# Prompt attention's exponentials over up to 1024 columns instead of 512

## The chip, the cores and the metric

One core of a Trainium2 chip runs the whole program. The metric is its device time in microseconds (us), from the profiler's and the runtime's clocks. Engines are named as in the profile: PE is TensorE (matmuls and transposes; PEld its weight loads), ACT is ScalarE, DVE is VectorE, POOL is GpSimd, SP is SyncE, which issues DMAs.

## What is computed

One layer of a streaming encoder, over 2048 prompt tokens and, separately, 64 sample tokens with a cache of 4096. Two groups of 8 heads look at the same tokens. The first is stick-breaking attention (a sigmoid of the scores and a running product instead of a softmax), the second is latent attention with a plain softmax over a mask in chunks of 64. The part that the change touches is the softmax of the prompt:

```python
s = (jnp.einsum('bqhn,bkhn->bhqk', q_nope, k_nope)
     + jnp.einsum('bqhr,bkr->bhqk', q_rope, k_rope)).astype(jnp.float32)
s = s * ((MLA_NOPE_DIM + MLA_ROPE_DIM) ** -0.5)
visible = (k_pos[None, :] // CHUNK) <= (q_pos[:, None] // CHUNK)
s = jnp.where(visible, s, jnp.finfo(jnp.float32).min)
p = jax.nn.softmax(s, axis=-1)
return jnp.einsum('bhqk,bkhv->bqhv', p.astype(v.dtype), v)
```

## The kernel before

The program is a row of phases: set-up, input projection, queries, keys, prompt attention (`prompt_attention_phase`, L1124), and a tail with the sample's attention and the output projection. A barrier of all engines closes each phase.

Prompt attention loops over 8 heads, and in each over two jobs: job 0 is stick-breaking, job 1 latent attention. The 2048 queries are 16 tiles of 128, in 4 groups (`g`, 4 tiles `i` each). A query tile's scores are computed against the keys that it may see, in chunks of 512 keys, so that group g has g+1 chunks per tile. This gives 4 x (1+2+3+4) = 40 chunks per job (`JOB`), 80 slots per head (`HEAD`), counted by `m`. Slots 0 to 39 are job 0, 40 to 79 job 1.

A second work runs 20 slots (`LEAD`) behind the scores: at slot `t` the finished weights of one block of 128 keys, for the 4 query tiles of a group, are transposed on TensorE (L1666), copied to a high part by ScalarE (`whi`, L1431), the remainder made a low part by VectorE (L1473), or by GpSimd (L1592) from a whole copy that ScalarE makes for it (L1436), and multiplied with the values 4 slots later (L1623). GpSimd has the low part where `on_pool(t)` holds: t of 60 to 79 and 0 to 19, but not where t % 4 is 3.

In each slot every engine runs its own fixed program, and semaphores join them. TensorE: the 4 transposes of t, the value matmuls of t - 4, then the scores of m = t + 20 (L1649 to L1655) into one of 2 banks, for which the scan or the maximum of m - 2 must be done. ScalarE: the copies of t, at the end of a group `finish` (L1424), then `chunk(h, m)`: in job 0 the sigmoid of chunk m (L1389), in job 1 the exponentials that `exps_at(m)` lists (L1396). VectorE: the low part of t - 1, then for m the scan (L1496, job 0) or the copy out of the bank with a running maximum (L1506, job 1), and after a tile's last chunk `negtop` (L1511).

An exponential needs the maximum of its whole row, so it runs in place on the tile `probs[g][i]` in SBUF after the tile's last chunk: piece c, of 512 columns, at one slot after the last chunk plus c. Slots at or over 80 fall into the next head: there the distance from 80 is halved, so that the four pieces of the last tile come as two at 80 and two at 81. At these, m is 0 and 1 of the next head, and ScalarE's `chunk` puts them ahead of that head's first sigmoids, both of which it runs at m = 1:

```python
if m < 2 and not (isinstance(h, int) and h == 0):
    for g, i, c in exps_at(HEAD + m):
        exp(h - 1, g, i, c)
    if m == 0:
        return
    sigmoid(h, 0)
```

Each piece gives its sum to its own column of `sums` (zeroed once at the start), which VectorE adds up over all 4 columns (L1518). A tile's last piece raises `exp_done`; TensorE waits for the 4 tiles of a group before that group's first transpose (L1663).

Of the kernel before, what the change touches and what calls it, by code (L numbers as in the profile page):

```python
# [11 lines left out]
P = 128  # L12
# [1111 lines left out]
def prompt_attention_phase(nc, outer, d, s, ps):  # L1124
# [4 lines left out]
    G = 4  # L1129
    GROUPS = 2 * G  # L1130
    CH = 512
    JOB = 40
    HEAD = 2 * JOB
# [4 lines left out]
    ADD = 4  # L1138
    PARTS = 4
    EVEN = 113  # L1140
    with ExitStack() as ctx:
        sb = lambda name, shape, dt=F32: ctx.enter_context(nc.sbuf_tensor(name, shape, dt))
        sm = Sems(nc, ctx, "pa")
# [45 lines left out]
        def upto(n):  # L1189

            g = n % G
            return JOB * (n // G) + 2 * (g + 1) * (g + 2)
# [5 lines left out]
        def chunk_of(m):  # L1198
            n, r = group_of(m)
            return n, *divmod(r, n % G + 1)  # L1200

        def keys_of(n, i, c):

            g = n % G
            kc = c if n >= G else g - c
            return kc * CH, (4 * g + i + 1) * P - kc * CH if kc == g else CH

        def first_query(t):
            n, i = group_of(t)
            return max(0, i - 4 * (n % G)) * P  # L1210

        def on_pool(t):

            return (t + LEAD) % HEAD < JOB and t % 4 != 3
# [3 lines left out]
        def low_of(h, t):  # L1218

            pool = on_pool(t)  # L1220
            per = POOLS if pool else HEAD - POOLS
            return (pool_lo if pool else dve_lo), per * (h + 1) + sum(on_pool(x) == pool for x in range(t + 1))
# [6 lines left out]
        def ends_at(t):  # L1229

            t = (t - LAG) % HEAD
            return next((n for n in range(GROUPS) if upto(n) % HEAD == t), None)

        def past(h, n):
            return h - 1 if n == GROUPS - 1 else h

        def is_none(h):
            return isinstance(h, int) and h < 0
# [13 lines left out]
        def chunk_at(h, t, last):  # L1252

            if t + LEAD < HEAD:
                return h, t + LEAD
            return (None, 0) if last else (h + 1, t + LEAD - HEAD)
# [13 lines left out]
        with nc.Block() as block:  # L1270

            @block.sync
            def _(sp):
# [31 lines left out]
                def load_v(h, job):  # L1305
# [9 lines left out]
                    if job == 0:  # L1315

                        sp.dma_start(step_v[:, 1:], v[P - 1:T - 1].rearrange("(j p) c -> p j c", p=P)).then_inc(v_loaded, 16)
                        sp.dma_start(step_v[1:EVEN, 0], v[0:EVEN - 1]).then_inc(v_loaded, 16)
                        sp.dma_start(step_v[EVEN:P, 0], v[EVEN - 1:P - 1]).then_inc(v_loaded, 16)

# [59 lines left out]
            @block.scalar  # L1380
            def _(act):
                act.sem_inc(taken, 2)
                act.sem_inc(whole_done, POOLS)
                def sigmoid(h, m):
                    n, i, c = chunk_of(m)
                    _, width = keys_of(n, i, c)
                    act.wait_ge(scores, HEAD * h + m + 1)
                    bank = ps[:, m % NS, 0:width]
                    act.activation(bank, bank, ACT.Sigmoid, scale=-SB_SCALE).then_inc(sig_done, 1)  # L1389

                def exp(h, g, i, c):
                    at = 4 * g + i
                    if c == 0:
                        act.wait_ge(negtop_done, 16 * h + at + 1)
                    keys = slice(c * CH, min((at + 1) * P, (c + 1) * CH))
                    x = act.activation(probs[g][i][:, keys], probs[g][i][:, keys], ACT.Exp, scale=MLA_SCALE,  # L1396
                                       bias=negtop[:, at:at + 1], accum_out=sums[:, at, c:c + 1])
                    if c == g:
                        x.then_inc(exp_done, 1)

                def exps_at(m):

                    due = [(m_last + 1 + c, g, i, c) for g in range(G) for i in range(4)
                           for m_last in (upto(G + g) - (3 - i) * (g + 1) - 1,) for c in range(g + 1)]
                    return [(g, i, c) for when, g, i, c in due if (when if when < HEAD else HEAD + (when - HEAD) // 2) == m]

                def chunk(h, m):
                    if h is None:
# [7 lines that stand above are left out]
                    if m < JOB:  # L1416
                        sigmoid(h, m)
                    for g, i, c in exps_at(m):
                        exp(h, g, i, c)

                def finish(h, n):
                    act.wait_ge(mixed, NW + HEAD * h + upto(n))
                    act.wait_ge(stored[n % 2], 16 * (G * h + n // 2))
                    act.activation(out[:, n % 2, :], ps[:, 6 + n % 2, :], ACT.Copy).then_inc(taken, 1)  # L1424

                def step(h, t, last):
                    q0 = first_query(t)
                    act.wait_ge(turned, HEAD * (h + 1) + t + 1)
                    act.wait_ge(mixed, HEAD * h + t + 1)
                    bank = ps[:, NS + t % NTB, q0:]  # L1430
                    act.activation(whi[:, t % NW, q0:], bank, ACT.Copy).then_inc(hi_done, 1)  # L1431
                    if on_pool(t):
                        before = (h, t - 4) if t >= 4 else (h - 1, HEAD + t - 4)
                        if on_pool(before[1]):
                            act.wait_ge(*low_of(*before))
                        act.activation(whole[:, t % 4, q0:], bank, ACT.Copy).then_inc(whole_done, 1)  # L1436
                    n = ends_at(t)
                    if n is not None and not is_none(past(h, n)):
                        finish(past(h, n), n)
                    if last and t + LEAD in (HEAD, HEAD + 1):  # L1440
                        for g, i, c in exps_at(t + LEAD):
                            exp(h, g, i, c)
                    chunk(*chunk_at(h, t, last))

                for m in range(LEAD):
                    chunk(0, m)
                act.wait_ge(own_loaded, 16)
                act.wait_ge(hide_made, 2)
                act.activation(own_tile[:], probs[3][2][:, 0:CH], ACT.Copy)
                act.activation(hide[:], probs[3][2][:, CH:CH + P + CHUNK], ACT.Copy).then_inc(const_done, 1)  # L1450
                steps_in_turn(act, step)
                finish(HEADS - 1, GROUPS - 1)
# [1029 lines left out]
```

## Time and profile before

| | us |
|---|---|
| median of 3 runs | 2436.88 (2432.28 to 2438.32) |
| the profiled execution | 2436.27 |
| its span, first to last instruction | 2434.2 |
| busy: TensorE, VectorE, ScalarE, GpSimd | 2196.4, 1344.1, 1323.2, 895.9 |
| prompt attention | from about 1016 to 2029 |

The span is what lies between the program's first and last instruction; the run's time has 2.07 us more around it. A row of a time line gives an instruction's start, its length, and in brackets how long its engine had been idle before it and what ended that. Rows of ScalarE overlap: one instruction ends after the next has begun, so what an instruction occupies is read from start to start. An exponential with a sum is two instructions, ACTIVATE and ACTIVATION_READ_ACCUMULATOR.

### The profile page before, as it was taken

Reading aid. Unit: us, or ns where it says so; the run is one execution under the profiler, and the core shown is the slowest. Engines: PE = TensorE matmul, PEld = TensorE weight load, DVE = VectorE, ACT = ScalarE, POOL = GpSimd, SP = SyncE. Lnnn points to the kernel's source line nnn. Section 1 sums busy time; section 2 is a strip of 40 time slices with the busy share of each in tenths; the row PEclk is TensorE's granted clock in tenths of the full one; section 3 lists DMA queues with packets and bytes.
Section 4 is the critical chain, followed back from the end, with each engine's and each line's share of the span. In section 5 each row is a group of like instructions: output and inputs, shape, how many; then the busy total and the mean of one; then the engine's idle time right before and its main releaser. Section 6 shows DMA issues by size and latency. Waiting matters only on the chain. (4 is left out here: it accounts for less than half of the span.)

```text
span 2434.2 us, 39766 instructions
## 1 busy us (share of the span) xinstructions
PE 2196.4 (90%) x12100; PEld 1837.8 (75%) x12100; DVE 1344.1 (55%) x2780; ACT 1323.2 (54%) x2872; POOL 895.9 (37%) x922
## 2 busy tenths in 40 slices
PE   6999997999988899789999999999999993999998
PEld 1888886999988577567777777777777782887876
DVE  3232322200138333387878787878787873667783
ACT  2232322211123333278888888888888884467553
POOL 0000000000000000265848484848484825656673
PEclk9999999999989999889999999999999996999999
DMA  7433342322347799943333323333323224676772
GB/s 274 136 98 99 96 123 72 126 72 93 115 155 198 247 320 312 259 90 83 78 84 69 87 67 87 70 87 71 86 70 89 47 64 123 189 227 185 218 211 87
DMA packets 296944, 320.16 MB, mean 132 GB/s; under 512 B 88641, under 2 KB 221788, under 8 KB 291826
## 3 DMA queue, kind: packets, MB, share of 16 engines
q1 hardware_dynamic: 292002, 302.00, 44.2%
q10 hardware_dynamic: 2880, 9.05, 1.0%
q0 software_dynamic: 1904, 7.41, 0.8%
q8 instruction: 51, 0.84, 0.1%
q14 instruction: 107, 0.88, 0.1%
HBM read 199.09 MB, written 110.90 MB: 127 GB/s over the span
## 5 line engine op out<-in xcount | busy, mean ns | idle before, releaser
L1431 ACT ACTIVATE pa_whi<-banks 128x512 fp32r<-128x512 f32 (+3 forms) x640 | 345.3, 540 | 99.1 <-PE banks L1666 80.3
L1666 PE MATMUL banks<-ident,pa_p 128*128 128x128 f32 x2176 | 356.4, 280 | 2.2 <-ACT pa_p L1396 2.2
L1649 PE MATMUL banks<-pa_khi,pa_qst 128*128 128x512 f32 (+3 forms) x640 | 261.0, 408 | 84.4 <-DVE pa_p L1496 76.5
L1592 POOL TENSOR_TENSOR pa_wlo<-pa_whole,pa_whi 128x512 fp32r<-128x512 f32 (+2 forms) x240 | 277.7, 1171 | 137.9 <-ACT pa_whole L1436 137.5
L1666 PEld LDWEIGHTS banks<-ident,pa_p 128*128 128x128 f32 x2176 | 269.2, 144 | 61.7 <-issue 5.2
L1623 PE MATMUL banks<-pa_whi,pa_vst 128*128 128x512 f32 (+3 forms) x640 | 286.3, 447 | 4.2 <-POOL pa_wlo L1592 3.0
L1496 DVE TENSOR_TENSOR_SCAN pa_p<-banks,pa_p,pa_zero 128x512 f32<-128x512 f32 x192 | 246.3, 1283 | 72.3 <-ACT banks L1389 65.7
L1473 DVE TENSOR_TENSOR pa_wlo<-banks,pa_whi 128x512 fp32r<-128x512 f32 (+3 forms) x400 | 234.8, 587 | 30.7 <-ACT pa_whi L1431 30.7
L1649 PEld LDWEIGHTS banks<-pa_khi,pa_qst 128*128 128x128 f32 x640 | 125.7, 196 | 159.1 <-DVE pa_p L1496 136.8
L1650 PE MATMUL banks<-pa_klo,pa_qst 128*128 128x512 f32 (+3 forms) x640 | 243.3, 380 | 0.0
L699 POOL DMA_DIRECT2D gate_ada<-in_ada_w_dram x2 | 1.8, 884 | 642.8 <-DVE qu_wlo L755 642.8
L1623 PE MATMUL banks<-pa_wlo,pa_vst 128*128 128x512 f32 (+3 forms) x640 | 237.9, 372 | 0.0
L1396 ACT ACTIVATE pa_p<-pa_p,pa_negtop 128x512 f32<-128x512 f32 (+2 forms) x320 | 208.8, 654 | 4.9 <-DVE pa_negtop L1511 4.3
L1389 ACT ACTIVATE banks<-banks 128x512 f32<-128x512 f32 (+3 forms) x320 | 172.0, 540 | 66.9 <-PE banks L1650 61.4
L653 PE MATMUL banks<-co_hhi,co_whi 128*128 128x352 f32 x576 | 188.1, 327 | 18.0 <-DVE co_h L620 9.8
L481 PE MATMUL banks<-nat_whi,pr_hhi 128*128 128x512 f32 (+5 forms) x544 | 196.1, 360 | 6.8 <-DVE pr_hlo L425 6.8
L481 PE MATMUL banks<-nat_wlo,pr_hhi 128*128 128x512 f32 (+5 forms) x544 | 195.3, 359 | 0.0
L481 PE MATMUL banks<-nat_whi,pr_hlo 128*128 128x512 f32 (+5 forms) x544 | 195.1, 359 | 0.0
L653 PE MATMUL banks<-co_hhi,co_wlo 128*128 128x352 f32 x576 | 186.0, 323 | 0.0
L1506 DVE TENSOR_SCALAR_CACHE_REDUCE pa_p<-banks,pa_top 128x512 f32<-128x512 f32 (+2 forms) x192 | 124.5, 648 | 30.4 <-PE banks L1652 17.9
L1650 PEld LDWEIGHTS banks<-pa_klo,pa_qst 128*128 128x128 f32 x640 | 127.2, 199 | 13.8
L1436 ACT ACTIVATE pa_whole<-banks 128x512 f32<-128x512 f32 (+2 forms) x240 | 136.6, 569 | 1.5 <-POOL pa_wlo L1592 1.5
(260 smaller groups left out, 5171.6 us busy)
## 6 DMA issues: line engine op xcount, KB each, us to landing
scratch_sb_kT<-ke_kT SPq DMA_DIRECT2D x12, 1024.0 KB, 8.9
scratch_mla_kT<-ke_nT SPq DMA_DIRECT2D x12, 1024.0 KB, 5.2
scratch_mla_v<-ke_v SPq DMA_DIRECT2D x12, 1024.0 KB, 5.4
scratch_gatesT<-co_gates SPq DMA_DIRECT2D x12, 704.0 KB, 11.3
ada<-in_ada_w_dram SPq DMA_DIRECT2D x4, 2048.0 KB, 11.9
pr_x<-in_x_prompt_dram SPq DMA_DIRECT2D x16, 512.0 KB, 18.1
scratch_hT<-pr_hT SPq DMA_DIRECT2D x16, 512.0 KB, 5.1
ke_k<-in_cache_sb_k_dram SPq DMA_DIRECT2D x8, 1024.0 KB, 7.7
```

The source lines that it names most:

```text
L481: mm = pe.matmul(ps[0:rows, 2 + g, 0:n], h[:, b, c, 0:rows], s[w][:, c, c0:c0 + n], start=(c == 0 and k == 0), stop=(c == DC - 1 and k == 2))
L653: mm = pe.matmul(ps[:, ct % RING, 0:N], w[:, c, ct * P:(ct + 1) * P], h[:, c, :], start=(c == 0 and k == 0), stop=(c == DC - 1 and k == 2))
L1389: act.activation(bank, bank, ACT.Sigmoid, scale=-SB_SCALE).then_inc(sig_done, 1)
L1396: x = act.activation(probs[g][i][:, keys], probs[g][i][:, keys], ACT.Exp, scale=MLA_SCALE, bias=negtop[:, at:at + 1], accum_out=sums[:, at ...
L1431: act.activation(whi[:, t % NW, q0:], bank, ACT.Copy).then_inc(hi_done, 1)
L1473: dve.tensor_tensor(wlo[:, t % NW, q0:], ps[:, NS + t % NTB, q0:], raw(whi[:, t % NW, q0:]), ALU.subtract).then_inc(dve_lo, 1)
L1496: dve.tensor_tensor_scan(tile[:, first_key:first_key + width][:, ::-1], scored[:, ::-1], given, start, ALU.mult, ALU.max).then_inc(scan_do ...
L1592: pool.tensor_tensor(wlo[:, t % NW, q0:], whole[:, t % 4, q0:], raw(whi[:, t % NW, q0:]), ALU.subtract).then_inc(pool_lo, 1)
L1623: mm = pe.matmul(ps[:, 6 + n % 2, q0:], vst[job][:, j, :], w[:, t % NW, q0:], start=(job == 1 and j == 0 and k == 0), stop=(j == 4 * g + 3 ...
L1649: pe.matmul(bank, qst[job][:, q], khi[job][:, keys], start=True, stop=False)
L1650: mm = pe.matmul(bank, qst[job][:, q], klo[job][:, keys], start=False, stop=(job == 0))
L1666: y = pe.transpose(ps[:, NS + t % NTB, x * P:(x + 1) * P], probs[g][x][:, i * P:(i + 1) * P], s["ident"][:])
```

## The change

A piece of an exponential covers up to 1024 columns (`WIDE`) instead of 512. A tile of group 0 and 1 then has one piece, a tile of group 2 and 3 two. Piece c still comes at one slot after the tile's last chunk plus c; the rule that halves the distance past slot 80 goes, since two pieces at 80 and 81 need no halving. `exp_done` is raised by the piece that ends at the tile's end. The copies, sigmoids, the order of the tiles and all other engines' programs stay as they are.

```diff
     EVEN = 113
+    WIDE = 2 * CH
...
-                    keys = slice(c * CH, min((at + 1) * P, (c + 1) * CH))
+                    keys = slice(c * WIDE, min((at + 1) * P, (c + 1) * WIDE))
                     x = act.activation(probs[g][i][:, keys], probs[g][i][:, keys], ACT.Exp, scale=MLA_SCALE,
                                        bias=negtop[:, at:at + 1], accum_out=sums[:, at, c:c + 1])
-                    if c == g:
+                    if keys.stop == (at + 1) * P:
                         x.then_inc(exp_done, 1)
 
                 def exps_at(m):
 
-                    due = [(m_last + 1 + c, g, i, c) for g in range(G) for i in range(4)
-                           for m_last in (upto(G + g) - (3 - i) * (g + 1) - 1,) for c in range(g + 1)]
-                    return [(g, i, c) for when, g, i, c in due if (when if when < HEAD else HEAD + (when - HEAD) // 2) == m]
+                    return [(g, i, c) for g in range(G) for i in range(4)
+                            for c in range(-(-(4 * g + i + 1) * P // WIDE))
+                            if upto(G + g) - (3 - i) * (g + 1) + c == m]
```

## Rows read from the trace of the kernel before

**Rows 1.** The page: the span, and busy time of each engine.

```profile
span 2434.2 us, 39766 instructions
PE 2196.4 (90%) x12100; PEld 1837.8 (75%) x12100; DVE 1344.1 (55%) x2780; ACT 1323.2 (54%) x2872; POOL 895.9 (37%) x922
```

**Rows 2.** Stretches: window, length, busy PE PEld DVE ACT POOL, clock, DMA share, GB/s.

```profile
1268.65:1330.40 61.75, 56.92 (x296) 43.84 (x297) 47.39 (x53) 50.60 (x109) 52.18 (x51) 0.92 0.31 72
1388.10:1392.70 4.60, 0.06 (x1) 0.00 (x0) 0.47 (x2) 4.57 (x13) 3.66 (x4) 0.80 0.09 21
...
sum 344.80, PE 344.72 PEld 298.17 DVE 294.66 ACT 287.48 POOL 144.06; mean PE 57.45 PEld 49.69 DVE 49.11 ACT 47.91 POOL 24.01
```

**Rows 3.** Waits in 1330 to 1388: who waits for whom, us, times, longest.

```profile
ACT pa_whi L1431 <- PE banks L1666: 9.1, 24, 0.7
DVE pa_p L1506 <- PE banks L1652: 4.6, 12, 0.6
```

**Rows 4.** Time line of TensorE at two of the seven junctions.

```profile
1392.71 0.69 PE L1649 MATMUL banks<-pa_khi,pa_qst 128*128 128x384 f32 x1 [4.55 <-DVE pa_p L1496]
...
1639.31 0.44 PE L1649 MATMUL banks<-pa_khi,pa_qst 128*128 128x384 f32 x1 [4.55 <-DVE pa_p L1496]
```

**Rows 5.** Time line of ScalarE, and VectorE's first scan, at one junction.

```profile
1385.89 0.60 ACT L1431 ACTIVATE pa_whi<-banks 128x512 fp32r<-128x512 f32 x1 [0.48 <-PE banks L1666]
...
1386.86 0.72 ACT L1396 ACTIVATE pa_p<-pa_p,pa_negtop 128x512 f32<-128x512 f32 x1
...
1387.57 0.72 ACT L1396 ACTIVATE pa_p<-pa_p,pa_negtop 128x512 f32<-128x512 f32 x1
...
1390.55 1.28 ACT L1389 ACT_TABLE_LOAD   x1
1391.85 0.54 ACT L1389 ACTIVATE banks<-banks 128x128 f32<-128x128 f32 x2
...
1392.23 1.00 DVE L1496 TENSOR_TENSOR_SCAN pa_p<-banks,pa_causal 128x128 f32<-128x128 f32 x2 [5.24 <-ACT banks L1389]
```

**Rows 6.** ScalarE by width: line, shape, count, busy us, mean ns, idle before.

```profile
L1431 ACT ACTIVATE pa_whi<-banks 128x512 fp32r<-128x512 f32 x320 | 193.3, 604 | 64.7 <-PE banks L1666 49.9 <-PE banks L1623 10.9
L1396 ACT ACTIVATE pa_p<-pa_p,pa_negtop 128x512 f32<-128x512 f32 x168 | 120.6, 719 | 1.8 <-DVE pa_negtop L1511 1.5
L1396 ACT ACTIVATION_READ_ACCUMULATOR pa_p<-pa_p,pa_negtop 128x1 f32 x240 | 46.4, 193 | 0.0
...
L1396 ACT ACTIVATE pa_p<-pa_p,pa_negtop 128x128 f32<-128x128 f32 x24 | 9.5, 395 | 0.1
...
L1947 ACT ACTIVATE ta_whi<-stage 128x1024 fp32r<-128x1024 f32 x8 | 8.4, 1046 | 0.0
```

**Rows 7.** Time line of TensorE and GpSimd at the end of the last head.

```profile
2002.80 0.66 PE L1666 MATMUL banks<-ident,pa_p 128*128 128x128 f32 x4 [2.22 <-ACT pa_p L1396]
...
2003.18 10.39 POOL L1592 TENSOR_TENSOR pa_wlo<-pa_whole,pa_whi 128x384 fp32r<-128x384 f32 x9
...
2016.21 5.38 POOL L1592 TENSOR_TENSOR pa_wlo<-pa_whole,pa_whi 128x512 fp32r<-128x512 f32 x5
```

**Rows 8.** A copy to the high part, and the low part that takes it.

```profile
1364.32 0.60 ACT L1431 ACTIVATE pa_whi<-banks 128x512 fp32r<-128x512 f32 x1
...
1365.99 0.69 DVE L1473 TENSOR_TENSOR pa_wlo<-banks,pa_whi 128x512 fp32r<-128x512 f32 x1
```

**Rows 9.** Stretches behind three restarts (the clock follows POOL's count); matmuls behind two stalls.

```profile
1145.10:1152.00 6.90, 6.86 (x37) 5.99 (x37) 3.66 (x6) 4.61 (x12) 4.49 (x5) 0.75 0.99 220
1268.60:1276.00 7.40, 7.35 (x29) 6.44 (x30) 3.36 (x5) 4.29 (x11) 4.08 (x5) 0.58 0.98 220
...
1884.50:1892.00 7.50, 7.46 (x37) 6.54 (x37) 3.73 (x6) 4.81 (x13) 4.67 (x5) 0.68 1.01 223
...
1401.27 0.50 PE L1649 MATMUL banks<-pa_khi,pa_qst 128*128 128x512 f32 x1 [0.72 <-DVE pa_p L1496]
...
1442.19 0.80 PE L1649 MATMUL banks<-pa_khi,pa_qst 128*128 128x512 f32 x1 [2.01 <-DVE pa_p L1496]
```

## The prediction

> **What bounds the kernel now.** I read the page first [rows 1]: TensorE is busy 90% of the span and ScalarE, whose instructions the change merges, 54%. These are averages over stages, so they don't say what a shorter ScalarE is worth. Next I cut the prompt attention into its two kinds of stretch with the table of stretches. A head has a stretch without exponentials (stick-breaking scores: sigmoid on ScalarE, scan on VectorE) and one with them (latent-attention scores). In six of the eight stretches with exponentials TensorE is busy 344.72 of 344.80 us at a granted clock of 1.00, which is the level of 2.4 GHz, and ScalarE 287.48 [rows 2]. In the stretch without them TensorE is busy 56.92 of 61.75 us [rows 2]. Then the waits of one exponential stretch [rows 3]: ScalarE waits 24 times for TensorE's transposes and VectorE's maxima wait for TensorE's scores; nothing of TensorE waits for ScalarE. So TensorE sets the pace where 36 to 40 of a head's 40 exponentials run, and nearly everything that is taken off ScalarE there becomes idle time of ScalarE.
>
> The exception is the junction where one head's last query tile is exponentiated and the next head's sigmoids begin. The table of stretches shows TensorE at 0.06 of 4.60 us there, and ScalarE at 4.57 [rows 2]. TensorE's time line has the stall: 4.55 us without a matmul, ended by VectorE's scan [rows 4]. It stands there seven times, once between each two heads, with the same 4.55 us. In the order of ScalarE around it [rows 5]: the copy of slot 60 starts at 1385.89 after 0.48 us of idleness that ended with a transpose, so up to there TensorE still leads. From there ScalarE has no gap: copies, two exponentials of 512 columns at slot m = 80, copies, two more at m = 81, the table load of 1.28 us, and at 1391.85 the sigmoids, to 1392.23 the first scan, and TensorE's stall ends at 1392.71. This chain is ScalarE's own work and it sets the time.
>
> **What an instruction costs.** The change turns a head's 40 exponentials (4x1, 4x2, 4x3, 4x4 pieces by group) into 24 (4x1, 4x1, 4x2, 4x2): 16 fewer per head, 128 in all, for the same elements. On ScalarE's line an exponential of 512 columns is followed by the next 0.71 us later, its accumulator read included, from 1386.86 to 1387.57 [rows 5]. The widths give the slope: 719 ns for 512 columns, 395 ns for 128 [rows 6], so 384 columns cost 324 ns and 512 more cost 432 ns. A piece of 1024 should take 0.71 + 0.43 = 1.14 us, and a merge saves 1.42 - 1.14 = 0.28 us. No exponential of 1024 columns is in the trace. Its bounds: it saves nothing (two of 512 cost 1.42), or it saves all that the rows count outside the columns, 719 + 193 - 432 = 480 ns. The nearest row for the width is a copy of 1024 columns at 1046 ns against 604 ns for 512 [rows 6]: 442 ns for the second 512, like the slope. So I take 0.28 us.
>
> The Trainium skill prices this otherwise: the page "ScalarE: Activation LUTs" (What ACT_TABLE_LOAD costs) gives about 280 ns plus 0.833 ns per element for an ACTIVATE with a pointer as bias, and an overlap of about 93 ns back to back, so 187 ns for each instruction saved. It doesn't price the accumulator's read, which these rows contain. By it the sum below would be 14 x 0.187 = 2.6 us, an estimate from that page.
>
> **Where the merges fall.** 128 x 0.28 = 36 us leave ScalarE. Of them:
>
> *The seven junctions.* The tile of m = 80 and 81 has four pieces of 512 and gets two of 1024, still one at each slot, behind the same copies. Two merges shorten the gapless chain by 0.56 us: the sigmoid, scan and matmul behind it come 0.56 us earlier, and the stall becomes 4.0 us. What is late next is still ScalarE, with its copies, 1.14 us twice, and the table load. The copies of slots 60 to 62 come earlier too, and nothing waits for them first. 7 x 0.56 = 3.9 us. After a junction all engines run in lockstep with TensorE's restart, so I let the whole shift pass on.
>
> *Inside the exponential stretches.* The remaining merges, and the removed table positions, are hidden by TensorE's 57.5 us of work per stretch: 0 us. If that cover were gone they would be worth the other 32 us.
>
> *The last head.* Here TensorE waits 2.22 us for the exponential itself [rows 7], the one place where a matmul does so. It would end 0.56 us earlier. But GpSimd's low parts run back to back from 2003.18 with 9, then the output's two instructions, then 5 to 2021.59 [rows 7], and the stage ends behind them. ScalarE's gain ends in front of GpSimd: 0 us. Without that cover it would be 0.56 us more.
>
> *Bursts.* A tile's first piece now takes 0.43 us more, and what follows on ScalarE, the copy to the high part, comes that much later; at a second piece of group 3 it adds up to 0.5 to 0.75 us, less ScalarE's idle time in between. Behind a late copy queue VectorE's low part and then its maximum, and for that TensorE's scores two slots on. In the tightest stretch (last tile of group 2, ScalarE without a gap) the copy starts at 1364.32, lasts 0.60, and VectorE takes it at 1365.99 [rows 8]: 1.07 us of room for 0.43. So 0 us.
>
> Nothing moves past a queue: no DMA, no sigmoid and no copy changes its place, and the pieces that move forward wait for the same maximum as the tile's first piece does now. The piece count of the sums falls, and the columns that aren't written stay at the zero of the start, at no time.
>
> Sum: 2436.27 us (the profiled execution: span 2434.2 and 2.07 around it) less 3.9 is 2432.4. The median of the runs, 2436.88, lies 0.6 above that execution, so 2433.0 us.
>
> **Rivals.** *The bursts starve TensorE* (slower). If VectorE took every late copy at once, a head would lose the first pieces' extra time: group 1 0.11 + 0.22 + 0.32 + 0.43, group 2 4 x 0.43, group 3's first three tiles 0.54 + 0.65 + 0.75, together 4.7 us; times 8 is 38 us, and less 3.9 that is 2471 us. It decides from the point where lateness exceeds the 1.07 us of rows 8, that is if a 1024-column piece takes over 1.8 us. Against it: that room, and ScalarE's idle time of up to 0.7 us per slot [rows 3]. Chance 0.05.
>
> *ScalarE is the pace after all*: 2436.9 - 36 = 2401 us. Against it is TensorE's 344.72 of 344.80 [rows 2]. Chance 0.03.
>
> *Width saves nothing* (it doesn't do what it says for the time): 2436.9 us. The copy of 1024 speaks against it. Chance 0.10.
>
> *The clock after the stall.* Each stall is followed by matmuls at 1.2 GHz for some microseconds, differently long: granted 0.75 over 6.9 us after one, 0.58 over 7.4 us after another [rows 9], 1.7 and 3.1 us of lost clock; for the seven restarts, of which three stand there, this adds to 15.2 us. A shorter stall falls differently in time. All seven like the best would give 3.3 us more, 2429.7 us; all like the worst would take 6.5 us, 2439.5 us; 0.08 each. That a stall of 4.0 us no longer lowers the clock would give 15.2 us, 2418 us; but after a stall of 2.01 us a matmul of 512 columns took 0.80 us against 0.50 us after one of 0.72 us [rows 9], so short ones lower it too. Chance 0.04.
>
> **How the numbers follow.** The forecast, 2433.0 us, has 0.62. With 0.28 us replaced by its bounds 0 and 0.48, the junctions give 0 to 6.7 us, 2436.9 to 2430.2 us. With the clock's two cases this makes a range of 2428.5 to 2439.5 us; outside are the starved TensorE, the two large gains and some tails, under 0.2. A measurement of this kernel can tell about 0.3%, 7.3 us, from no change, so the forecast counts as the same. Faster by more: 0.03 + 0.04, half of the good clock case, and a tail of the forecast, 0.14. Slower by more: 0.06. Same: 0.80.
>
> **What would show it.** In the changed kernel's trace: 192 exponentials, those of 1024 columns at about 1.14 to 1.15 us; seven stalls of 4.0 us where 4.55 us stood; exponential stretches still filled by TensorE and as long as now; a last head whose GpSimd ends as late after its start as now. I am wrong if the stalls keep 4.55 us, if VectorE's low part begins to wait for ScalarE's copy inside an exponential stretch, if those stretches shorten, or if the last head passes its 0.56 us on.

## The result, and the profile after

The changed kernel took 2443.32 us (median of 10 runs, 2437.58 to 2451.85) against 2434.47 us (10 runs, 2428.73 to 2440.47) of the kernel before beside it: ratio 1.0035, 95% interval 1.002 to 1.005. The forecast was 2433.0 us, at most 2439.5. So the kernel is some 8.5 us slower, although about 36 us of work, by the forecast's price, are gone from ScalarE. In the changed kernel's file all lines from the attention on are one higher than before (L1389 is L1390, L1396 is L1397, L1431 is L1432, L1496 is L1497, L1649 is L1650).

The page of the changed kernel, to hold against [rows 1]:

```profile
span 2439.6 us, 39510 instructions
PE 2198.1 (90%) x12100; PEld 1840.7 (75%) x12100; DVE 1345.5 (55%) x2780; ACT 1280.6 (52%) x2616; POOL 895.7 (37%) x922
```

ScalarE has 256 instructions fewer, 128 exponentials and their accumulator reads, and is busy 42.6 us less. Its time line at one junction answers to [rows 5], TensorE's next to it to [rows 4] (start, length, and in brackets the idle time before):

```profile
1383.08 1.15 ACT L1397 ACTIVATE pa_p<-pa_p,pa_negtop 128x1024 f32<-128x1024 f32 x1
1384.12 0.20 ACT L1397 ACTIVATION_READ_ACCUMULATOR pa_p<-pa_p,pa_negtop 128x1 f32 x1
1384.21 0.49 ACT L1432 ACTIVATE pa_whi<-banks 128x384 fp32r<-128x384 f32 x1
...
1384.95 1.16 ACT L1397 ACTIVATE pa_p<-pa_p,pa_negtop 128x1024 f32<-128x1024 f32 x1
...
1386.23 1.28 ACT L1390 ACT_TABLE_LOAD   x1
```

```profile
1388.38 0.44 PE L1650 MATMUL banks<-pa_khi,pa_qst 128*128 128x384 f32 x1 [4.00 <-DVE pa_p L1497]
```

From start to start an exponential of 1024 columns with its read takes 1.13 us, from 1383.08 to 1384.21, and the stall is 4.00 us at all seven junctions instead of 4.55. That is what was forecast. So are the exponential stretches, which the table of stretches shows full of TensorE as in [rows 2] (first, and sum of six):

```profile
1203.40:1260.10 56.70, 56.70 (x350) 49.05 (x348) 48.43 (x137) 42.34 (x92) 25.48 (x31) 1.00 0.42 92
...
sum 345.68, PE 345.60 PEld 299.14 DVE 295.68 ACT 259.54 POOL 157.35; mean PE 57.60 PEld 49.86 DVE 49.28 ACT 43.26 POOL 26.23
```

ScalarE fell there from 287.48 to 259.54 us and nothing came of it, as said. What is new stands in the other stretch, in its middle. In the kernel before, TensorE stalled once per head there, for 1.79 to 2.11 us; one of the six, 2.01 us, is in [rows 9]. In the changed kernel it stalls 2.79 to 3.20 us. The rows of ScalarE and TensorE in the first of these, before and after:

```profile
1191.52 0.60 ACT L1431 ACTIVATE pa_whi<-banks 128x512 fp32r<-128x512 f32 x1 [2.43 <-PE banks L1623]
...
1194.03 0.50 PE L1649 MATMUL banks<-pa_khi,pa_qst 128*128 128x512 f32 x1 [2.11 <-DVE pa_p L1496]
```

```profile
1187.79 0.60 ACT L1432 ACTIVATE pa_whi<-banks 128x512 fp32r<-128x512 f32 x1 [3.17 <-PE banks L1624]
...
1190.30 0.50 PE L1650 MATMUL banks<-pa_khi,pa_qst 128*128 128x512 f32 x1 [2.85 <-DVE pa_p L1497]
```

The profile puts ScalarE's idle time down to a matmul of L1623 (L1624). The waits of the window 1200 to 1900 name it so five times, before and after:

```profile
ACT pa_whi L1431 <- PE banks L1623: 10.9, 5, 2.3
```

```profile
ACT pa_whi L1432 <- PE banks L1624: 16.6, 5, 3.5
```

What these waits share is a branch. The loop over heads (`steps_in_turn`, L1240 to L1249) turns at slot 12 of the next head, in the middle of that stretch. Branches are no busy time in the profile, but the trace records them: in the kernel before, ScalarE's next instruction after its jump back comes 2.39 to 2.75 us later in the six turns, in the changed kernel 3.15 to 3.54 us. VectorE's comes 2.95 to 3.23 us later in both, GpSimd's and SyncE's 0.3 us; at the loop's exit, where ScalarE's jump isn't taken, 0.08 us. In the changed kernel's rows above, ScalarE jumps at 1184.40 and its sequencer goes on at 1187.58; TensorE's last matmul there had ended at 1187.44, so the copy at 1187.79 waited for the jump and not, as the label says, for the matmul.

A part of the loss lies just ahead of the jump. In the kernel before, ScalarE's branch starts 0.07 us behind the start of the last sigmoid ahead of it, in the changed kernel 0.35 us. From that sigmoid's start to the first instruction behind the jump it is 2.46 to 2.82 us before and 3.49 to 3.90 us after, on average 1.06 us more, and six times that is the 6.4 us by which the middle stalls grow in the table below.

The stretch from the first to the seventh junction, cut by TensorE's own stalls (us; the last column is the time at half clock in it, from the start of the first junction's stall to that of the seventh):

| kernel | stretch | six junction stalls | six middle stalls | half clock |
|---|---|---|---|---|
| before | 739.4 | 27.3 | 11.5 | 47.8 |
| changed | 744.3 | 24.0 | 17.9 | 54.6 |

These are one execution each; a second execution of the kernel before has 44.4 us at half clock.

### The profile page after: what moved, and what is told of

It reads as the page before. It is cut to its first block and busy times, and to the rows that moved or that the text cites. A ratio compares the mean times of both kernels' runs of the same rounds, so it can differ in the third digit from the quotient of the medians.

```text
span 2439.6 us, 39510 instructions
## 1 busy us (share of the span) xinstructions
PE 2198.1 (90%) x12100; PEld 1840.7 (75%) x12100; DVE 1345.5 (55%) x2780; ACT 1280.6 (52%) x2616; POOL 895.7 (37%) x922
## 5 line engine op out<-in xcount | busy, mean ns | idle before, releaser
L1432 ACT ACTIVATE pa_whi<-banks 128x512 fp32r<-128x512 f32 (+3 forms) x640 | 344.0, 538 | 144.8 <-PE banks L1667 123.9
L1650 PE MATMUL banks<-pa_khi,pa_qst 128*128 128x512 f32 (+3 forms) x640 | 262.0, 409 | 85.9 <-DVE pa_p L1497 78.4
L1624 PE MATMUL banks<-pa_whi,pa_vst 128*128 128x512 f32 (+3 forms) x640 | 286.4, 448 | 4.8 <-POOL pa_wlo L1593 3.6
L1497 DVE TENSOR_TENSOR_SCAN pa_p<-banks,pa_p,pa_zero 128x512 f32<-128x512 f32 x192 | 246.4, 1283 | 73.0 <-ACT banks L1390 67.1
L1474 DVE TENSOR_TENSOR pa_wlo<-banks,pa_whi 128x512 fp32r<-128x512 f32 (+3 forms) x400 | 234.9, 587 | 30.0 <-ACT pa_whi L1432 18.1
L1650 PEld LDWEIGHTS banks<-pa_khi,pa_qst 128*128 128x128 f32 x640 | 126.1, 197 | 160.6 <-DVE pa_p L1497 137.3
L1624 PE MATMUL banks<-pa_wlo,pa_vst 128*128 128x512 f32 (+3 forms) x640 | 237.0, 370 | 0.0
L1390 ACT ACTIVATE banks<-banks 128x512 f32<-128x512 f32 (+3 forms) x320 | 171.8, 539 | 68.4 <-PE banks L1651 62.6
L653 PE MATMUL banks<-co_hhi,co_whi 128*128 128x352 f32 x576 | 188.2, 327 | 17.1 <-DVE co_h L620 9.8
L1397 ACT ACTIVATE pa_p<-pa_p,pa_negtop 128x1024 f32<-128x1024 f32 (+2 forms) x192 | 172.7, 899 | 4.9 <-DVE pa_negtop L1512 4.4
L1507 DVE TENSOR_SCALAR_CACHE_REDUCE pa_p<-banks,pa_top 128x512 f32<-128x512 f32 (+2 forms) x192 | 124.5, 649 | 30.4 <-PE banks L1653 17.9
L1497 DVE TENSOR_TENSOR_SCAN pa_p<-banks,pa_causal 128x128 f32<-128x128 f32 (+3 forms) x128 | 103.7, 816 | 63.7 <-ACT banks L1390 61.4
```

The source lines that it names most:

```text
L653: mm = pe.matmul(ps[:, ct % RING, 0:N], w[:, c, ct * P:(ct + 1) * P], h[:, c, :], start=(c == 0 and k == 0), stop=(c == DC - 1 and k == 2))
L1474: dve.tensor_tensor(wlo[:, t % NW, q0:], ps[:, NS + t % NTB, q0:], raw(whi[:, t % NW, q0:]), ALU.subtract).then_inc(dve_lo, 1)
L1497: dve.tensor_tensor_scan(tile[:, first_key:first_key + width][:, ::-1], scored[:, ::-1], given, start, ALU.mult, ALU.max).then_inc(scan_do ...
L1624: mm = pe.matmul(ps[:, 6 + n % 2, q0:], vst[job][:, j, :], w[:, t % NW, q0:], start=(job == 1 and j == 0 and k == 0), stop=(j == 4 * g + 3 ...
L1650: pe.matmul(bank, qst[job][:, q], khi[job][:, keys], start=True, stop=False)
```

## Theories

**Theory L (the jump's place).** 32 instructions per turn (16 exponentials and 16 reads) left ScalarE's loop, so the jump moved in its program. In the compiled program an instruction is 64 bytes. ScalarE's loop begins at instruction 591 in both kernels; the jump is number 1066 before and 1034 after. The trace shows the engines' code arriving in packets of its own kind of queue, of 8192 bytes (128 instructions) on this queue: in the changed kernel 0.87 MB in 106 packets over the span.

```profile
q14 instruction: 106, 0.87, 0.1%
```

1066 lies 42 instructions behind a multiple of 128, 1034 lies 10 behind one. In the kernel before, the last packet fetched in sequence had come about 7 us ahead of the jump, and the first fetch after the jump starts 0.9 us behind it. In the changed kernel a packet starts 0.67 us behind the jump, two more at about 1.5 and 1.6, and two at about 4. The packet at 0.66 us is also there at the loop's exit, where nothing is jumped to: so it is the next one in sequence, which by this theory was asked for just before the jump and goes ahead of the target's. VectorE jumps 0.4 to 0.7 us behind ScalarE and its packets come over the same queue, so which of the later ones is whose isn't shown.

By that, the trace agrees with what the Trainium skill says in "Runtime: NRT & Kernel Launch" (Instruction fetch mechanics): instructions are prefetched in sequence only, and a taken branch whose target isn't in the engine's two-page window waits for a fetch. The page puts no price on it and says nothing of the jump's place. Its blocks are of 16 KiB; the packets of this queue are of 8192 bytes, and the measurement decides.

**Rivals.** B: something in the wide pieces themselves (bursts, order) makes the kernel late. N: it is chance, a difference between executions. The expectations below use these letters; those of the later parts use M, N, C and D for other rivals and say which.

## The experiments

A filler below is `act.sem_inc(passed, 1)` on a semaphore that nobody waits for: one instruction of code, 0.07 us apart from the next. Ratios are to the kernel before on the same chip.

### The jump's place

**The changed kernel and the kernel before again**, unaltered, as a base.

> The changed kernel itself, on the chip of the runs beside it. In its profile the stall between two heads shrank from 4.55 to 4.00 us as predicted, but the stall in the middle of each stick-breaking stretch grew from 1.8 to 2.1 us to 2.8 to 3.2 us. It stands where the loop over the heads jumps back: ScalarE's next instruction came 2.4 to 2.75 us after the branch before the change and 3.15 to 3.5 us after it. Theory L (layout): the 32 instructions that the loop body lost moved ScalarE's branch to 10 instructions behind a multiple of 128 (1034 instead of 1066 in the compiled program); there a sequential fetch of 8 KB, which is 128 instructions, is still under way when the branch asks for its target. L expects 3.15 to 3.5 us again, and +6 to +10 us against before. Theory B (bursts): the longer exponentials delay ScalarE so that the loss is in the exponentials' stretches; B expects stretches longer than 57.5 us. Theory N (noise between executions): no difference beyond 3 us.

> The kernel before, profiled once more, for its tail: in the two profiles with pieces of 512 the phase behind prompt attention took 402.0 and 402.3 us, in the four with wide pieces 405.0 to 407.0. If that belongs to the change, this profile shows 402 again; if it is a matter of one execution, anything from 402 to 407 can come.

Measured: 2443.67 us, ratio 1.0036 (1.0021 to 1.0051), the jump 3.22 to 3.55 us, middle stalls 18.1 us in all; and for the kernel before one run of 2439.05 us, middle stalls 11.5 us, the jump 2.39 to 2.79 us. So rival N falls. The phase behind prompt attention took 405.9 us in this run of the kernel before, and 400.9 to 407.0 us in the kernels with a short junction: its length belongs to the execution and not to the change.

**Padded by 32.** The jump is back at 1066.

```diff
+                FILLERS = {47: 2, 49: 2, 51: 2, 53: 2, 57: 2, 60: 2, 63: 2, 66: 2,
+                           70: 4, 74: 4, 78: 4, 79: 4}
...
                     for g, i, c in exps_at(m):
                         exp(h, g, i, c)
+                    for _ in range(fillers_at(m)):
+                        act.sem_inc(passed, 1)
```

> The changed kernel with 32 fillers (a semaphore increment that nobody waits for) in ScalarE's loop body, two for each exponential that is gone, in slots in which ScalarE idles. The branch is at 1066 again. L expects 2.4 to 2.75 us at the branch as before the change, stalls of 4.00 us between heads, and a time 3 to 5 us under before (the predicted 3.9), so 8 to 12 us under the changed kernel. B and N expect the changed kernel's time.

Measured: 2433.81 us, ratio 0.9997 (0.9986 to 1.0007), 9.9 us below the changed kernel. ScalarE's jump takes 2.39 to 2.79 us again, the middle stalls 12.3 us, with the exponentials as wide as in the changed kernel:

```profile
1188.97 0.60 ACT L1440 ACTIVATE pa_whi<-banks 128x512 fp32r<-128x512 f32 x1 [2.34 <-PE banks L1632]
...
1191.48 0.50 PE L1658 MATMUL banks<-pa_khi,pa_qst 128*128 128x512 f32 x1 [2.02 <-DVE pa_p L1505]
```

32 added instructions made the kernel faster, and rival B falls. What didn't come is the rest of the expectation, 3 to 5 us under the kernel before.

**The kernel before, with 96 fillers.** Its jump goes to 1162, which is again 10 behind a multiple of 128.

```diff
+                    if 68 <= m < 80:
+                        for _ in range(8):
+                            act.sem_inc(passed, 1)
```

> The kernel before the change, with its exponentials of 512 columns, and 96 of the same fillers in ScalarE's loop body, so that the branch is at 1162, again 10 behind a multiple of 128. L expects 3.15 to 3.5 us at the branch although nothing of the exponentials changed, and 5 to 9 us over before. B and N expect the time of before; fillers that cost by themselves would show in the exponentials' stretches, where they are.

Measured: 2451.6 us, ratio 1.0069 (1.0053 to 1.0086). The jump takes 3.14 to 3.64 us, the middle stalls 18.2 us instead of 11.5, at narrow exponentials. The mechanism is as expected; the price, 17 us, is twice to three times what was expected. Half clock rises to 54.6 us in that stretch. What the fillers cost by themselves can be in the price too; no run separates it.

**Padded by 16** (`FILLERS = {70: 4, 74: 4, 78: 4, 79: 4}`), the jump at 1050, 26 behind a multiple.

> The changed kernel with 16 fillers: the branch at 1050, 26 behind the multiple. If the fetch at the boundary is over about 3 us after the boundary was passed, as its packet's place in the changed kernel's trace says (0.67 us behind a branch that stands 10 instructions behind the boundary), L expects 2.4 to 2.75 us here too, and the time of the kernel with 32 fillers within 2 us. If the length of the body matters in proportion, it expects half of the loss, 2.9 us at the branch.

Measured: 2437.01 us, ratio 1.0005 (0.9994 to 1.0016), jump 2.39 to 2.63 us, middle stalls 11.4 us. The median is 3.2 us above that of the kernel padded by 32, where at most 2 were expected, but the two intervals overlap. Half the padding brings the jump and the stalls back whole, so it is a step between 10 and 26, not a price per instruction of distance.

**The same body, a longer prologue.** 32 fillers ahead of the loop and none in it, so both its ends move by 32.

```diff
+                    if m < 16:
+                        act.sem_inc(passed, 1)
+                        act.sem_inc(passed, 1)
```

> The changed kernel with the 32 fillers ahead of ScalarE's loop instead of in it: the body stays 442 instructions long, the branch stands at 1066, 42 behind a multiple of 128, the loop's begin at 623, 17 instructions ahead of one. If the branch's position decides, ScalarE resumes after 2.4 to 2.8 us; if the shorter body is what costs, after 3.15 to 3.5 us. The target close ahead of a boundary may bring a second wait 17 instructions further on, of up to 1 us; time 2433 to 2441 us by the first, 2443 us by the second.

Measured: ratio 1.0007 (0.9995 to 1.002), jump 2.39 to 2.75 us, middle stalls 11.4 us. The place decides and not the body's length. And the unit is 128 instructions: 1034 and 1162 are both slow and both 10 behind a multiple of 128, but 1162 is not 10 behind a multiple of 256.

Why the place costs is argued, not shown by itself. What speaks for the sequential fetch is that it starts 0.65 to 0.99 us behind the jump in the two slow kernels, while in the others it had come well ahead: 3.2 to 3.5 us at 26 instructions, 6.8 to 7.2 us at 42.

**VectorE's own jump.** It stands at 1024, on a multiple of 128, and costs 3.0 us in every kernel. One kernel adds 16 fillers to its loop (the edit below), one 20 ahead of the loop; both are the kernel padded by 32 otherwise.

```diff
+                    if 40 <= t < 56:
+                        dve.sem_inc(passed, 1)
```

> The changed kernel with 32 fillers on ScalarE, and 16 in VectorE's loop body too, whose branch stood exactly on a multiple of 128 (1024, now 1040). L expects VectorE to resume 2.4 to 2.75 us after its branch instead of 3.0 to 3.25; TensorE's stall of 2.0 us shrinks by at most 0.3 us, since ScalarE's sigmoid, 1.3 us behind ScalarE's own resumption, then decides. If the position against the multiple doesn't matter to VectorE, it stays at 3.0.

> The changed kernel with 32 fillers on ScalarE, and 20 on VectorE ahead of its loop, so that VectorE's loop begins at 659, 19 behind a multiple of 128, instead of 639, the last instruction ahead of one. Adding 16 in the body left VectorE's 3.0 us as it was. If the 3.0 us come from the target (one instruction of the first block, and then a wait for a second block), VectorE resumes after about 2.4 us now; if not, 3.0 us stays. TensorE's mid-stall is decided by ScalarE in either case, so 2430 to 2437 us.

Measured: ratios 0.9995 (0.9984 to 1.0006) and 0.9997 (0.9984 to 1.0011); VectorE's jump still takes 2.96 to 3.31 us. So neither its jump's nor its target's place explains its 3.0 us. That stays open.

### What the jumps cost in all

**ScalarE without a jump back**: in ScalarE's program of the changed kernel the loop over heads is written out.

```diff
-                steps_in_turn(act, step)
+                for h in range(HEADS):
+                    for t in range(HEAD):
+                        step(h, t, h == HEADS - 1 and t >= TURN)
```

> The changed kernel with the head loop written out on ScalarE alone; VectorE still jumps back and resumes 3.0 to 3.25 us later. If ScalarE's branch alone made the mid-stall, it goes away (2415 us as with both written out). If VectorE's jump costs as much by itself, TensorE still stalls for 1.5 to 2 us there: VectorE resumes 3.0 us after its branch, does a low part and a scan, and TensorE waits for the scan; then 2425 to 2432 us. I expect the second.

Measured: 2425.4 us, ratio 0.9961 (0.9943 to 0.9979). Middle stalls of 1.66 to 1.76 us remain, 10.2 us in all, now by VectorE's jump. They are only some 1.6 us shorter in all than those of the kernels with ScalarE's jump at its old cost, but the stretch from the first to the seventh junction is 8 us shorter (728.7 against 736.9 us, the mean of eight executions), and in it the clock costs 18.8 us instead of 25.6 (half of the time at half clock is lost): only one of the six stalls is followed by half clock. Most of what this edit gives comes by the clock.

**Both written out**, once with wide and once with narrow exponentials.

> The changed kernel with the loop over the heads written out on ScalarE and VectorE, so that neither jumps back. Theory L expects no stall of TensorE over 1 us in the middle of the stick-breaking stretches (12.3 us of them in the kernel with 32 fillers), stalls of 4.00 us between heads as ever, and 12 to 17 us less than the kernel with 32 fillers, 2417 to 2422 us. If the wait was not the branch's, the stalls of 2 us stay.

> The kernel before with the same loops written out: pieces of 512, no back edge. Between this and the run with wide pieces nothing differs but the width, and no layout of a loop's end. The prediction's step (two merges of 0.28 us on the chain of each of seven junctions) expects the wide one 3.9 us faster, stalls of 4.00 against 4.55 us; the theory that bursts cost something elsewhere expects less than that or the reverse; a tail that depends on the width would take 4 us back and leave 0.

Measured: wide 2415.34 us, ratio 0.9917 (0.99 to 0.9934); narrow 2417.86 us, ratio 0.9929 (0.9913 to 0.9946). No middle stall above 1 us is left in either. The junctions, wide and then narrow:

```profile
1145.36 0.69 PE L1654 MATMUL banks<-pa_khi,pa_qst 128*128 128x384 f32 x1 [3.84 <-DVE pa_p L1499]
```

```profile
1143.25 0.69 PE L1653 MATMUL banks<-pa_khi,pa_qst 128*128 128x384 f32 x1 [4.39 <-DVE pa_p L1498]
```

Without the two engines' jumps the kernel before is 17 us faster, the clock's part included (it runs at 0.958 instead of 0.955), about four times what the change was to give at the junctions. Without them the change is worth 2.5 us where 3.9 were forecast; the two intervals overlap, so that alone proves neither a gain nor its loss. The wide kernel with both written out is the fastest of the study, and it beats both kernels.

### Where the junctions' 3.9 us went

With the jump restored the wide kernels should lie 3.9 us below the kernel before. They lie level. Two rivals to the saving passing on (L) for this: what the junction saves is given back behind it (M), or the wide pieces inside the stretches cost something (N in these texts). To tell them apart one kernel has wide pieces at the junction's tile alone, one everywhere else (`!=` for `==`); in both the jump is at 1066, by 4 fillers in the one and 28 in the other.

```diff
+                def piece_of(g, i):
+                    return WIDE if (g, i) == (3, 3) else CH
...
-                    keys = slice(c * WIDE, min((at + 1) * P, (c + 1) * WIDE))
+                    piece = piece_of(g, i)
+                    keys = slice(c * piece, min((at + 1) * P, (c + 1) * piece))
```

> The changed kernel with only the tile that stands at the junction between heads (query group 3, key group 3) in pieces of up to 1024 columns, all others in pieces of 512 as before, and with 4 fillers in ScalarE's loop, so that ScalarE's jump back stands at the same position of its code as in the kernel before. Theory L (position of the jump, and the junction's saving passes on): junction stalls 4.0 us instead of 4.55, mid-stretch stalls 1.8 to 2.1 as before, time 2.5 to 4 us below the kernel before. Rival M (what the junction saves is given back later by whatever paces the stretch behind it): junction stalls 4.0 as well, but the time within 1 us of the kernel before.

> The changed kernel with the junction's tile alone in pieces of 512 and all others in pieces of up to 1024, with 28 fillers, so that ScalarE's jump back stands at the same position as before. Theory L: junction stalls 4.55 us and mid-stretch stalls 1.8 to 2.1 as before, and the time within 1 us of the kernel before, since merges inside stretches that TensorE paces are worth nothing. Rival N (the wide pieces inside the stretches cost something, for TensorE waits longer for freed banks): 2 to 3 us above the kernel before, and the stretch between the first and the seventh junction longer by as much outside the stalls.

> The changed kernel with 32 fillers once more, the same program as in the earlier run with its jump back padded to its old position, now beside the two kernels that merge at the junction alone and everywhere else. Theory L: 2.5 to 4 us below the kernel before, as the junction-only kernel; rival M: within 1 us of the kernel before, as the junction-only kernel; rival N: 2 to 3 us above the junction-only kernel.

Measured: the junction's tile alone 2435.19 us, ratio 1.0 (0.999 to 1.0009), with stalls of 4.00 us; all but it 2435.89 us, ratio 0.9998 (0.9988 to 1.0008), stalls 4.55 us; the kernel padded by 32 again, ratio 0.9997 (0.9987 to 1.0007). So 112 merges inside the stretches cost nothing and bring nothing, as forecast, and the 14 at the seven junctions (two more are in the last head), which do shorten the stall, bring nothing either: L and N fall, and M, a saving given back, holds.

It is given back in the clock. Each run has a mean granted clock of TensorE. Over the runs of the experiments, and for the changed kernel those of the result too (means, with standard errors):

| kernels | junction stall | runs | us | mean granted clock |
|---|---|---|---|---|
| before | 4.55 | 115 | 2435.6 ± 0.3 | 0.9551 ± 0.0002 |
| all wide but the junction's tile | 4.55 | 12 | 2435.3 ± 0.6 | 0.9555 ± 0.0004 |
| wide at the junction, jump takes 2.4 to 2.9 us | 4.0 | 92 | 2435.2 ± 0.3 | 0.9536 ± 0.0002 |
| changed | 4.0 | 17 | 2443.8 ± 0.8 | 0.9526 ± 0.0004 |

The third row has seven kernels (the one padded by 32 twice), those with the jump's cost restored, one of the next part among them. Set against the kernel before on the same chip, their clock is lower in all five groups of runs, on average by 0.0017 ± 0.0002, and their time by 0.5 ± 0.4 us. 0.9551 less 0.9536 is 0.0015, and 0.0015 of 2435 us is 3.7 us, an upper bound, since it holds if TensorE had work all the time. It balances nearly all of the junctions' 7 x 0.55 = 3.85 us; measured is a difference of 0.4 us. The place is seen in the stretches. These are the 10 us behind the six middle stalls, their clock the number ahead of the last two; first the kernel with a wide tile at the junction only (first and last of the six), then the one with wide tiles everywhere else (all six):

```profile
1192.72:1202.72 10.00, 9.94 (x48) 7.86 (x49) 7.85 (x7) 8.93 (x18) 9.67 (x10) 0.83 0.16 40
...
1807.19:1817.19 10.00, 9.93 (x48) 7.81 (x49) 7.84 (x7) 8.93 (x18) 9.67 (x10) 0.83 0.16 40
```

```profile
1192.02:1202.02 10.00, 9.51 (x54) 7.18 (x54) 8.60 (x8) 9.56 (x19) 9.67 (x10) 1.00 0.16 40
1314.64:1324.64 10.00, 9.41 (x53) 7.10 (x53) 8.53 (x8) 9.58 (x19) 9.67 (x10) 1.00 0.16 40
1437.19:1447.19 10.00, 9.44 (x53) 7.13 (x54) 8.54 (x8) 9.59 (x19) 9.67 (x10) 1.00 0.17 40
1559.85:1569.85 10.00, 9.93 (x48) 7.80 (x49) 7.90 (x7) 8.90 (x18) 9.67 (x10) 0.83 0.17 40
1683.00:1693.00 10.00, 9.93 (x49) 7.78 (x49) 8.03 (x7) 9.05 (x18) 9.67 (x10) 0.85 0.16 40
1805.70:1815.70 10.00, 9.42 (x53) 7.12 (x53) 8.55 (x8) 9.58 (x19) 9.67 (x10) 1.00 0.16 40
```

The stalls ahead of these are of one kind in both, 1.86 to 2.15 us in the first kernel and 1.81 to 2.09 in the second. Yet with the short junction all six are followed by matmuls at 1.2 GHz for part of the 10 us (0.83), with the long one only two of six. Over the profiled executions it is 45 of 48 (eight with a short junction) against 10 of 18 (three with a long one). TensorE does 54 matmuls in such 10 us at 1.00, and 48 at 0.83.

Half of the time at half clock is lost. Summed from each stall's start to 12 us behind its end, the clock costs 9.6 us at the six middle stalls with the short junction (mean of the eight) and 5.7 us with the long one (mean of the three), 3.9 us more, while behind the junctions it costs as much in both (16.0 and 15.9 us). The six junction stalls are 3.3 us shorter, and the stretch shrinks by only 0.8 us (737.7 to 736.9). The two kernels with both loops written out have no middle stall, and there it was behind the junctions that the wide one lost more, 17.1 us against 11.9; but that is one execution of each.

**What of the junction does it?** Two kernels more, both the one padded by 32 with fillers moved: ten to ahead of the next head's first sigmoid, to hold the junction at its old length; or eight to right behind the jump, to hold the middle stall and bring the head back to its old length with a short junction.

```diff
+                        for _ in range(10):
+                            act.sem_inc(passed, 1)
                         sigmoid(h, 0)
```

> The changed kernel with 32 fillers and the jump back at its old position, as in the padded kernel before it, but 10 of the fillers stand at the junction, ahead of the next head's first sigmoid, so that the junction lasts about as long as in the kernel before although its exponentials are wide. Theory C (what the shorter junction saves is taken back by the clock, because the stalls then fall otherwise in time): junction stall 4.3 to 4.6 us, mean granted clock back at about 0.955 as in the kernel before and the one with a narrow junction tile (0.9552, 0.9555), the head's middle stall at half clock in about half of the heads, and the time still 2434 to 2437 us. Rival D (the wide pieces themselves lower the clock): clock 0.9535 and time 2438 to 2440 us.

```diff
+                    if t == TURN:
+                        for _ in range(8):
+                            act.sem_inc(passed, 1)
```

> The padded changed kernel with 8 of its 32 fillers right behind the jump back instead, which holds the middle stall of each head for about 0.5 us more; junction stall 4.0 us. The head then lasts as long as in the kernel before (123.2 us from junction to junction), but with the time in the middle. Theory C in the form that the head's length decides: clock back at about 0.955 and time 2434 to 2437 us. In the form that the junction's own length decides: clock at 0.9535 or below, and time 2438 to 2440 us.

Measured: the first held nothing. The fillers ran in the shadow of the exponentials, the stall stayed at 4.00 us, and the kernel is one of its kind again: 2434.73 us, ratio 1.0 (0.9991 to 1.0009), all six middle stalls followed by 0.83 or 0.84. Theory C's condition wasn't met, and the run doesn't separate the junction's length from the width of its pieces. The second did what it was to do (middle stalls 14.9 us in all, the stretch 739.2 us, as long as before's 739.4), took 2437.81 us, ratio 1.0007 (0.9998 to 1.0016), and still had 0.83 to 0.84 behind all six. So a head of the old length doesn't bring the clock back behind these stalls, with the reserve that they are also longer here, 2.32 to 2.77 us. Its mean granted clock, 0.9540, and its time fit neither form of the theory well: the kernel before has 0.9547 ± 0.0004 beside it. Nor is the short junction enough by itself: with ScalarE's loop alone written out the junction is short too, 3.93 us, and of its six middle stalls of 1.66 to 1.76 us only one was followed by half clock. Which property of the shorter junction makes the next stall lower the clock is open.

## Why the prediction was wrong, point by point

- **TensorE sets the pace where the exponentials run; merges there are worth 0.** Right: the kernel with wide pieces everywhere but at the junction has a ratio of 0.9998.
- **A merge saves 0.28 us; a piece of 1024 takes 1.14 us.** Right: 1.13 us from start to start. The slope over widths carried to a width that the trace didn't have.
- **Seven stalls go from 4.55 to 4.0 us.** Right to the hundredth.
- **The last head gives 0.** Right. Its stall before the transposes fell from 2.22 us [rows 7] to 1.68 us, and GpSimd's row of nine low parts is as long as before:

```profile
2004.39 10.39 POOL L1593 TENSOR_TENSOR pa_wlo<-pa_whole,pa_whi 128x384 fp32r<-128x384 f32 x9
```

- **Bursts cost 0.** Right: VectorE has no wait for a copy in the exponential stretches that it didn't have before, and they are full of TensorE.
- **"The remaining merges, and the removed table positions, are hidden by TensorE's 57.5 us of work per stretch: 0 us"** and **"Nothing moves past a queue".** Here it failed. The sum counted what the removed instructions cost while they run and left out what they are as code. Taking 32 of them out of ScalarE's loop moved its jump from 42 to 10 instructions behind a multiple of 128, and the jump's cost from between 2.39 and 2.75 us to between 3.15 and 3.54 us, with 0.28 us more just ahead of it, six times, with TensorE stalled by it. That is 6.4 us of stall (17.9 less 11.5). The stall itself stood in [rows 9] with 2.01 us, as a witness for the clock; that I never asked what ended it is the error before this one. Its cause, had it been asked, was a loop turning there. What a place costs stood in no row, but a rival could have been named: an edit of the loop's length moves the jump, at a price of some tenths of a us to about 1 us per turn.
- **"After a junction all engines run in lockstep with TensorE's restart, so I let the whole shift pass on."** Wrong too. The stalls shortened, and the clock behind the next stall took it back: 3.85 us gained, up to 3.7 us lost, with 3.9 us more lost behind the six middle stalls in the profiled executions. The clock was among the rivals, but only behind the junctions themselves, as a matter of chance with both signs. Over many runs it has one sign, and its place is the next stall, in the middle of the head.

The sum by these terms: -3.85 us at the junctions, +6.4 at the jumps, and at most +6.1 by the clock (0.0025 of 2435 us, between 0.9551 and 0.9526), together at most +8.7 us. Measured over all runs: 2443.8 - 2435.6 = +8.2 us. The clock's term is an upper bound, so the sum allows the measured time and doesn't prove the split. Of the rivals none was this; the one on the slow side, starved TensorE, had another mechanism and place.

## What to carry to other kernels

Before an edit inside a hardware loop, find where the loop turns and which engine stalls there: the profile may put that stall down to another engine's instruction. If the jump is on the path, compare the kernel with one of the same loop length (fillers), before the edit is judged; better, write out the loop in the engines on the path, which here was worth 17 us. And where TensorE's clock falls after each stall, 0.5 us off a stall is no gain until runs have shown it: judge it by the mean granted clock beside the time.

## What was unexpected of the hardware

- A taken jump back costs ScalarE 2.4 to 2.8 us and VectorE 3.0 to 3.3 us until its next instruction, GpSimd and SyncE 0.3 us, TensorE's sequencer 0.02 us; ScalarE's untaken one 0.08 us. A turn is 474 recorded instructions on ScalarE (442 in the changed kernel), 384 on VectorE, but 180 on GpSimd and 113 on SyncE. With ScalarE's jump 10 instructions behind a multiple of 128 it was 3.14 to 3.64 us (two kernels, eighteen turns), at 26 and at 42 it was 2.39 to 2.87 us.
- Adding 32 instructions without any use to ScalarE's loop made the changed kernel 9.9 us faster; 96 made the kernel before 17 us slower.
- Stalls of about the same length (1.75 to 2.23 us) are followed by half clock in nearly all heads (45 of 48) or in about half of them (10 of 18), depending on whether the junction some 47 us earlier lasted 4.0 or 4.55 us. Stalls of 1.66 to 1.76 us were so in one of six.
- Ten fillers behind an exponential cost ScalarE nothing that could be seen: they ran while it was computing.
